# Loading the second tile of x and the second norm row later, and moving VectorE's position operations behind the second tile's low parts

## The reference, cut to what matters

```python
h = rms_norm(x, norm_mix_pre[i])
z = h @ w_in[i]
dist = jnp.abs(pq[..., :, None] - pw[..., None, :]).astype(jnp.float32)
```

## Time and profile before

| | |
|---|---|
| median of 3 runs | 2010.19 us (2009.0 to 2010.32) |
| profiled execution | 2010.66 us, its span 2009.0 us |
| TensorE matmuls busy | 1949.5 us, 97% of the span |
| VectorE busy | 1103.9 us, 55% |
| ScalarE busy | 958.4 us, 48% |
| GpSimd busy | 178.3 us, 9% |
| HBM read | 330.47 MB |

### The profile page before, as it was taken

One profiled execution on the slowest core, in us unless ns is written; L12 is line 12 of the kernel. 1 busy time (PEld: TensorE's weight loads), 2 busy tenths in 40 slices (PEclk: granted clock), 3 DMA queues, 4 the chain that ended last, 5 costly groups with the idle time before them and its releaser, 6 DMA issues.

```text
span 2009.0 us, 26183 instructions
## 1 busy us (share of the span) xinstructions
PE 1949.5 (97%) x9072; PEld 1572.0 (78%) x9072; DVE 1103.9 (55%) x1330; ACT 958.4 (48%) x1256; POOL 178.3 (9%) x262
## 2 busy tenths in 40 slices
PE   7999999998999999999899999999999999999998
PEld 6777878886877787887788877688878888767886
DVE  5565665556566565445655554554465555555444
ACT  4554454445546445444544444644454444555443
POOL 4310010001421000000200022000011000100000
PEclk9999999999999999999999999999999999999999
DMA  6234555554513445554555553265555554434552
GB/s 213 95 105 152 185 192 188 188 188 139 168 61 119 179 171 189 188 188 170 192 192 186 185 187 129 85 203 186 188 181 199 188 188 166 158 105 147 188 188 105
DMA packets 204844, 332.73 MB, mean 166 GB/s; under 512 B 11344, under 2 KB 150224, under 8 KB 204752
## 3 DMA queue, kind: packets, MB, share of 16 engines
q1 hardware_dynamic: 200240, 319.33, 47.4%
q0 software_dynamic: 3120, 11.02, 1.7%
q10 hardware_dynamic: 1392, 1.21, 0.2%
HBM read 330.47 MB, written 1.05 MB: 165 GB/s over the span
## 4 chain that ended last, share of the span: by engine, by line
PE 61%; issue 32%; DVE 4%; ACT 2%; POOL 1%; DMA 1%; POOLq 0%; SPq 0%; ACTq 0%; DVEq 0%
PE ps L501 18%; PE ps L505 17%; PE ps L503 17%; PE ps L663 3%; PE ps L513 2%; PE ps L676 1%; PE ps L699 1%; PE ps L687 1%; DVE wlo L1583 1%; ACT whi L1138 1%; DMA raw<-w_in_dram 1%; POOL stat L2093 1%; POOL stat L2094 0%; DVE h L1627 0%; DVE act_lo L1589 0%
## 5 line engine op out<-in xcount | busy, mean ns | idle before, releaser
L1583 DVE TENSOR_TENSOR wlo<-raw,whi 128x2048 fp32r<-128x2048 f32 (+1 forms) x304 | 686.0, 2257 | 542.3 <-ACT whi L1138 542.2
L1138 ACT ACTIVATE whi<-raw 128x2048 fp32r<-128x2048 f32 (+2 forms) x308 | 581.0, 1886 | 433.3 <-PE ps L505 429.1
L501 PE MATMUL ps<-whi,act_hi 128*128 128x512 f32 (+1 forms) x1632 | 619.1, 397 | 15.3 <-DVE wlo L1583 8.1
L505 PE MATMUL ps<-whi,act_lo 128*128 128x512 f32 (+1 forms) x1632 | 607.2, 390 | 0.0
L503 PE MATMUL ps<-wlo,act_hi 128*128 128x512 f32 (+1 forms) x1632 | 606.7, 389 | 0.0
L501 PEld LDWEIGHTS ps<-whi,act_hi 128*128 128x128 f32 x1632 | 305.8, 189 | 80.9 <-issue 17.7
L505 PEld LDWEIGHTS ps<-whi,act_lo 128*128 128x128 f32 x1632 | 307.8, 189 | 64.9
L503 PEld LDWEIGHTS ps<-wlo,act_hi 128*128 128x128 f32 x1632 | 308.2, 189 | 60.0
L1182 ACT ACTIVATE hid<-ps,stat 128x256 f32<-128x256 f32 x132 | 62.7, 475 | 283.9 <-PE ps L513 200.1
L2093 POOL TENSOR_TENSOR stat<-stat,eps 128x1 f32<-128x1 f32 x44 | 34.6, 785 | 1520.9 <-ACT prob L1169 1520.8
L501 PE MATMUL ps<-whi,hid_hi 128*128 128x512 f32 x496 | 153.4, 390 | 0.0
(11 more groups left out here) (201 smaller groups left out, 1811.9 us busy)
## 6 DMA issues: line engine op xcount, KB each, us to landing
raw<-ffn_w_gate_dram SPq DMA_DIRECT2D x88, 512.0 KB, 4.0
raw<-ffn_w_up_dram SPq DMA_DIRECT2D x88, 512.0 KB, 5.1
raw<-ffn_w_down_dram SPq DMA_DIRECT2D x88, 512.0 KB, 3.9
raw<-w_in_dram SPq DMA_DIRECT2D x64, 512.0 KB, 4.4
raw<-w_ffn_gate_dram SPq DMA_DIRECT2D x44, 512.0 KB, 4.0
raw<-w_ffn_up_dram SPq DMA_DIRECT2D x44, 512.0 KB, 5.0
raw<-w_ffn_down_dram SPq DMA_DIRECT2D x44, 512.0 KB, 3.8
raw<-a_w_qkv_dram SPq DMA_DIRECT2D x24, 512.0 KB, 4.4
```

The source lines that it names most:

```text
L501: nc.tensor.matmul(o, hi, a, start=start, stop=False)
L505: last = nc.tensor.matmul(o, lo, a, start=False, stop=stop)
L1138: nc.scalar.activation(whi[:, u % SLOTS, 0:words], raw[:, u % SLOTS, 0:words], ACT.Copy)\
L1583: nc.vector.tensor_tensor(wlo[:, u % SLOTS, 0:words], raw[:, u % SLOTS, 0:words], whi[:, u % SLOTS, 0:words].bitcast(F32), ALU.subtract)\
```

## The change

ScalarE issues the load of the second tile of x after the square of the first tile, behind its other loads. GpSimd issues the load of gain row 1 behind the angle operations. VectorE makes the low parts of tile 1 and of unit 2 ahead of the position operations instead of behind them. No instruction is added or taken away.

```diff
             act.dma_start(gains[:, 0, :], ...).then_inc(s_in["gain"], 16)
-            act.dma_start(xs[:, 1, :], A["x"][0, P:S, :]).then_inc(s_in["x1"], 16)
             act.dma_start(posk[:, :], ...).then_inc(s_in["pos"], 16)
...
             act.wait_ge(s_in["x0"], 16)
             square(0, xs[:, 0, :])
+            act.dma_start(xs[:, 1, :], A["x"][0, P:S, :]).then_inc(s_in["x1"], 16)
             turned_rows_hi(TN_MIX, (0,))
...
             dve.wait_ge(s_in["x1"], 16)
             nc.vector.tensor_tensor(ht[:, 1, :], xs[:, 1, :], gains[:, 0, :], ALU.mult).then_inc(sem("h_ready"), 1)
             split(2)
+            turned_rows_lo(TN_MIX, 1)
+            split(1)
...
             assert n_parts[0] == DISTANCE_STEPS
-            turned_rows_lo(TN_MIX, 1)
-            split(1)
             with dve.Fori(0, DEPTH) as li:
...
             inverse(0)
-            load_gain(1, 1)
...
             assert n_table[0] == ANGLE_STEPS
+            load_gain(1, 1)
 
             pool.wait_ge(s_parts, DISTANCE_STEPS)
```

## The result

| | before | changed |
|---|---|---|
| median of 20 runs | 2009.72 us (2008.12 to 2010.73) | 2014.24 us (2011.5 to 2016.62) |
| ratio, 95% interval | | 1.0023 (1.0016 to 1.003) |
| profiled execution | 2010.66 us | 2013.78 us |

The changed kernel is slower, by 4.5 us in the medians. The forecast of 2015.9 is 1.7 us too high; as a change, 5.75 us was forecast and 4.5 came. That it is slower at all is clear, since the interval stays above 1.

The account below looks back on a forecast made before the run. TensorE, busy 97% of the span, bounds the kernel; its start is limited by the second weight unit's landing. A 4.05 us later c = 1 plus a 1.7 low-clock stretch gave 5.75, median 2015.9; own range 2014.6 to 2017.2, full 2011.2 to 2018.2.

Parts of the forecast that it names:

- x1 lands at 15.4: ScalarE's queue: the second tile of x, behind 960 small packets taking 6.1 us, lands at 15.4 instead of 8.3.
- the rival that it is not held up: ScalarE's queue: x1 lands by 11 us, ahead of VectorE's need; 2011.0 to 2012.7, not slower; chance 0.12.
- turns of 9 to 17 descriptors: DMA queues: by the skill's rule a turn would clear a dozen small rows at once and hardly hold up x1.
- First matmul 19.05: TensorE's start: first matmul of weight unit 0 at 19.05 instead of 15.54, behind VectorE's wait for x1.
- One low stretch of 1.7 us ahead of the turns: TensorE before the second tile's turns: 4.3 us idle, then the clock at its lower level, costing 1.7 us.
- The positions cost 4.0 ahead of z_half, the stall is 2.9: VectorE: position operations directly ahead of z_half(0, 0) cost 4.0 us; TensorE stalls 2.9 us before z's second column part.
- c = 1: TensorE: second column part of z, forecast to start at 35.6 instead of 31.54, +4.05 us.
- A low stretch behind the stall, +1.7: TensorE after the 2.9 us stall: one more stretch at the lower clock, adding 1.7 us.
- Nothing of this comes back later.: After the start: later work has slack, with 16 us left to GpSimd and VectorE after the positions.
- The norm row: Gain row 1, 512 KB out of the start: second weight unit lands between 13.6 and 15 instead of 16.3, gain not cashed.
- the rival in which the clock stays up behind the stall: TensorE behind the stall: x1 late but no second low stretch, +4.05 us, 2014.2; chance 0.16.
- the 0.2% bound: Whole kernel: 0.2%, 4.0 us, is told from no change; slower begins at 2014.2, given 0.67.

Follow-up runs that it names:

- e4: Changed kernel with the small rows of cs2 issued behind the second tile of x on ScalarE's queue; +2.8 us against before, ratio 1.001.
- e8: Changed kernel with the load of gain row 1 back ahead of the angles on GpSimd; +7.1 us against before, ratio 1.0037.
- e6: Changed kernel with VectorE making the low parts of weight units 0 and 1 ahead of its wait for x1; +1.2 us against before, ratio 1.0004.
- e5: Changed kernel with 76 warming transposes on TensorE instead of 36; +3.1 us against before, ratio 1.0016.
- e9: Changed kernel repeated word for word for a second trace, a single execution; took 2014.57 us.
- e10: Changed kernel repeated for a third trace, a single execution; took 2014.33 us.
- e11: Kernel before the change, repeated for a second trace, a single execution; took 2009.19 us.
- e1: Changed kernel with the load of x1 back as second on ScalarE's queue; +2.1 us against before, ratio 1.0007.

## Why the prediction was right, point by point

- **x1 lands at 15.4.** Right: 15.57. The pace was 172 packets per us instead of 156, and x1 still took its own 1.95. The order on the queue as the cause is shown by e4, though it gave half of its expected size, and the number of queues by e8; the rival that it is not held up did not come. The prediction had tied that rival to the turns of 9 to 17 descriptors in the Trainium skill ("DMA: Bandwidth & Descriptors", "Queues, rings and completion order"). Neither half of that argument stands. Turns of that size for both queues would have given equal counts too, and would have held x1 up just as long. What speaks against such turns are the distances of 6 and 80 ns between single packets: here the turns are in the main one row long.
- **First matmul 19.05.** Right: 19.14. e6 shows the step behind it, that VectorE's wait is what carries the delay.
- **One low stretch of 1.7 us ahead of the turns.** Mis-sized in the first trace: it was 6.8 us long, 5.7 of them under matmuls, and cost 2.6 (e5). The turns came at 26.00 instead of 24.85. In e9 and e10 it was 3.4 us long and cost 1.6, and the turns came at 24.94 and 24.66.
- **The positions cost 4.0 ahead of z_half, the stall is 2.9.** Right: 31.76 to 35.7 and a stall of 2.62 (2.65, 2.63). c = 1 was forecast at 35.6; it came at 36.50, 35.44 and 35.17.
- **A low stretch behind the stall, +1.7.** Absent in the first trace, present in e9 and e10. The forecast for the first 50 us, 5.75, stands against 5.1, 5.6 and 5.4 us at the latents' turns. In the first trace it is partly luck that the sum comes near: one stretch was twice as long as forecast and the other absent.
- **"Nothing of this comes back later."** Right where the later low stretches are the same: e9 and e10 against e11 keep 5.4 and 5.1 of the 5.8 and 5.5 us. In the first pair of traces it is otherwise. There the changed kernel has two later low stretches where the kernel before has four, and the distance falls from 4.98 us at the matmul after 280 us to 3.1 at 1222. The medians differ by 4.5, about 1 less than the marks. That they fall short for this reason is argued, not shown; it would take the clock of many executions.
- **The norm row.** Its gain was said not to be cashed. That is right for the second weight unit, which nobody waited for, but incomplete: e8 shows that without the move x1 would have landed 1.55 us later and c = 1 started 1.7 us later. The sum had that inside the landing of x1. That the row had time till about 40 us to land was right: it landed at 30.0.

The median of 2014.24 lies inside the full range (2011.2 to 2018.2) but below the forecast's own (2014.6 to 2017.2). It is the number of the rival in which the clock stays up behind the stall (2014.2), and the first trace did go that way, though with a longer stretch before. Two of three traces have the forecast's two stretches. So the mechanism holds in each step, the size is 1.2 us too large as a change, and the outcome fell only narrowly on the slower side of the 0.2% bound.

## What to carry to other kernels

On a queue of transfers, count rows, not bytes: 960 small packets ahead of a load held it up for microseconds, since the two queues took turns row by row. Count the small rows behind it too: 307 of them went before the load in e4 had landed. A late load is free as long as nothing else stands behind the wait for it; put the wait behind the work that doesn't need it (e6 took 4 us off the first matmul with the same transfers). And before moving a block of small operations out of an idle time, look for what stands next on that engine and which bank it must empty: the same 4 us were free in one place and a stall of 2.6 in the other.

## What the runs showed of the hardware that was not expected

- The low clock behind an idle time of 2 to 3 us isn't certain: with an idle time of 2.59 us near 285 us there was no low stretch in the first trace of the changed kernel and one in e9 and e10. Nor is its length set by the idle time. The low stretches of these starts came in two lengths, 3.4 and 6.8 us, and behind idle times of 2.79 and 2.80 us it was 3.4 in e6 and 6.8 in e1.
- Filling an idle time of 4.7 us with 40 more transposes kept the clock up and delayed the first matmul by no more than 0.2 us (e5).
- Two queues with rows of 2 KB and of 4 to 64 bytes took turns one row each (6 and 80 ns between the starts, 172 rows per us and queue), and rows of a transfer issued later on the same queue went before the last rows of an earlier one (e4, 307 of 528).
- A small operation of GpSimd that meets VectorE's low-part subtraction (2.3 us, two inputs in SBUF) takes 1.7 to 2.5 us instead of 0.2 to 0.6 and ends just behind it, in all thirteen traces. Which operation is hit changes with the schedule: the second inverse in the changed kernel, four of the angle operations in e7. It is a coincidence in time seen 42 times, and no run took the subtraction away.
